# Stick-breaking attention: the eight heads worked in pairs instead of one after the other

## The reference, cut to what matters

```python
z = q @ k.T * hd ** -0.5
mask = key_pos < q_pos                       # strictly earlier keys
log_1mb = where(mask, log_sigmoid(-z), 0.0)
later = reverse_cumsum(log_1mb) - log_1mb    # over the keys
w = where(mask, exp(log_sigmoid(z) + later), 0.0)
out = w @ v
```

## Time and profile before

| | us |
|---|---|
| median of 3 runs (2521.0 to 2522.18) | 2521.75 |
| the profiled execution, its own time | 2521.97 |
| its span from first to last instruction | 2520.0 |
| first logits of the stage (L1310) | 1810.53 |
| copy of the last head's output (L2843) | 1923.59 |
| from one to the other | 113.06 |

### The profile page before, as it was taken

The page is one execution under the profiler, slowest core; times in us unless marked ns, Lnnn a source line. Parts: engine busy times, 40 slices in busy tenths (PEclk is TensorE's granted clock), DMA queues, the critical chain, the costliest instruction groups (busy, mean ns, idle before and its releaser), DMA issues.

```text
span 2520.0 us, 32191 instructions
## 1 busy us (share of the span) xinstructions
PE 2410.5 (96%) x12056; PEld 2069.8 (82%) x12056; DVE 1341.5 (53%) x1855; ACT 912.2 (36%) x1439; POOL 1087.3 (43%) x879
## 2 busy tenths in 40 slices
PE   5999889999999999999999999999888999999999
PEld 5899789999999998766788888888754766788887
DVE  7757866746565644889641222557444332543433
ACT  4222332313131323777632332345544343322322
POOL 1533132534444432378644567844520422444444
PEclk8999999999999999999999999999999999999999
DMA  6434012423333231411222322322300211232223
GB/s 246 150 101 140 28 59 70 149 101 117 117 109 114 102 111 43 132 33 44 69 84 92 104 97 80 113 84 92 117 17 6 76 59 56 78 101 93 100 92 109
DMA packets 71910, 232.04 MB, mean 92 GB/s; under 512 B 9824, under 2 KB 14048, under 8 KB 71776
## 3 DMA queue, kind: packets, MB, share of 16 engines
q1 hardware_dynamic: 71776, 230.16, 27.5%
HBM read 218.00 MB, written 2.10 MB: 87 GB/s over the span
## 4 chain that ended last, share of the span: by engine, by line
PE 78%; DVE 7%; POOL 5%; issue 5%; ACT 3%; DMA 1%; SPq 1%; POOLq 0%; DVEq 0%; ACTq 0%
PE PS L792 57%; PE PS L810 8%; PE PS L833 3%; POOL HL L592 2%; PE PS L1324 2%; POOL XR L634 1%; DVE RD L2640 1%; POOL PL L634 1%; PE PS L1425 1%; SPq L474 1%; PE PS L1310 1%; DMA EARLY<-adastream 1%; DVE OG L2454 1%; DVE SM L2624 1%; PE PS L892 0%
## 5 line engine op out<-in xcount | busy, mean ns | idle before, releaser
L592 POOL TENSOR_TENSOR HL<-RAW,HL 128x512 fp32r<-128x512 f32 x614 | 872.9, 1443 | 1303.9 <-ACT HL L1468 1302.7
L792 PE MATMUL PS<-HID,HL 128*128 128x384 f32 (+1 forms) x2832 | 562.1, 359 | 0.6 <-DVE HID L2196 0.6
L792 PE MATMUL PS<-HA,HL 128*128 128x512 f32 (+2 forms) x2592 | 552.0, 365 | 8.8 <-DVE VA L2563 2.3
L792 PEld LDWEIGHTS PS<-HID,HL 128*128 128x128 f32 x2832 | 509.5, 188 | 51.5 <-DVE HID L2196 1.1
L792 PE MATMUL PS<-HB,HL 128*128 128x512 f32 (+2 forms) x2592 | 538.9, 359 | 0.0
L792 PEld LDWEIGHTS PS<-HA,HL 128*128 128x128 f32 x2592 | 464.3, 189 | 74.4 <-issue 22.6
L792 PEld LDWEIGHTS PS<-HB,HL 128*128 128x128 f32 x2592 | 462.9, 188 | 50.7
L1468 ACT ACTIVATE HL<-RAW 128x1024 fp32r<-128x1024 f32 x307 | 323.3, 1054 | 476.4 <-PE PS L792 383.8
L2252 DVE CUSTOM_DVE_ANT_0 ADJ<-ADA,CB 128x1024 f32<-128x1024 f32 x160 | 264.3, 1652 | 12.8 <-DVE X L2172 5.2
L2172 DVE SCALAR_TENSOR_TENSOR X<-PS,MOD,X 128x256 f32<-128x256 f32 (+1 forms) x160 | 80.7, 546 | 285.2 <-PE PS L792 271.9
L2201 DVE TENSOR_TENSOR T<-T 128x768 f32<-128x768 f32 (+1 forms) x64 | 72.8, 1137 | 197.7 <-ACT T L1529 197.5
(11 more groups left out here) (421 smaller groups left out, 2583.4 us busy)
## 6 DMA issues: line engine op xcount, KB each, us to landing
RAW<-wstream SPq DMA_DIRECT2D x307, 512.0 KB, 3.3
ADA<-adastream SPq DMA_DIRECT2D x80, 512.0 KB, 3.8
EARLY<-adastream SPq DMA_DIRECT2D x16, 512.0 KB, 14.6
QB<-QH SPq DMA_DIRECT2D x32, 128.0 KB, 2.3
X<-x_in SPq DMA_DIRECT2D x8, 384.0 KB, 6.7
QC<-QL SPq DMA_DIRECT2D x16, 128.0 KB, 2.3
out<-X SPq DMA_DIRECT2D x8, 256.0 KB, 2.0
X<-mem SPq DMA_DIRECT2D x1, 1024.0 KB, 5.7
```

Source lines behind the costliest of these rows:

```text
L592: a = pool.tensor_tensor(HL[:, t % RING, 1, half], RAW[:, t % RAW_RING, half], HL[:, t % RING, 0, half].bitcast(F32), ALU.subtract)
L792: mm = pe.matmul(PS[:, bk, 0:hi - lo], w[:, wp, k * P:(k + 1) * P], a[:, ap, lo:hi], start=(k == 0 and (wp, ap) == (0, 0)), stop=(k == nk ...
```

## The change

- Heads are worked in pairs c = (2c, 2c+1), called a = 0 and a = 1. `sb_bank` gives six banks to a pair: block 0 of the two heads in banks 0 and 1, block 1 in banks 2 and 3, block 2 of both in bank 4, block 3 of both in bank 5.
- `logits(c)` issues the eight logit products of the pair so that head a = 0 (lower array half) and a = 1 (upper half) alternate, and two neighbours never go to the same bank. It starts when the weights of blocks 3 and 2 of the pair before are read, and waits inside for blocks 1 and 0. Eight masks follow.
- `later(c, 0)` and `later(c, 1)` are the same ten products each.
- ACT does six `Abs` (two of head 1, four of head 0), `Exp` and `Ln` of head 0, the other two `Abs`, `Exp` and `Ln` of head 1, and then the `Exp` of both heads' weights.
- DVE writes softplus over `AB` in place; the weights go to new tiles `WT`, so `SPB` goes.
- `values(c)` issues the eight products of the pair alternating between the two column halves, one pair late, and waits for all eight weights. `pair_out` copies them.
- The SSM has bank 7 alone: `state_in` comes in four parts of 8 passes. Parts 1 and 2 and `state_out(0)` stand between the last `later` of a pair and the next logits; part 3, `lag_products` and `state_out(1)` stand behind `values` in a pair.
- POOL computes its powers before the low parts of tiles `T_OUT2` to +2, and ACT makes one high part after each of the first three pairs. SP loads tile `T_OUT2` + 2 before the `LAG` moves and + 3 after them, and + 4 after the y moves.

```diff
+        SB_BANK, SB_COL = [(0, 1), (2, 3), (4, 4), (5, 5)], [(0, 0), (0, 0), (0, 256), (0, 128)]
+        def sb_bank(a, i, lo, hi=NX):
+            return PS[:, SB_BANK[i][a], SB_COL[i][a] + lo - i * P:SB_COL[i][a] + hi - i * P]
+        SB_LOGITS = [(0, 3), (1, 2), (0, 1), (1, 1), (0, 0), (1, 0), (1, 3), (0, 2)]
+        SB_MASKS = [(0, 3), (1, 3), (0, 2), (1, 2), (0, 1), (0, 0), (1, 1), (1, 0)]
...
+            def logits(c):
...
+                if c:
+                    pe.wait_ge(S("sb_weights"), 8 * c - 2)
+                for n, (a, i) in enumerate(SB_LOGITS):
+                    if c and n in (2, 4):
+                        pe.wait_ge(S("sb_weights"), 8 * c - n % 4 // 2)
+                    if n == 6:
+                        pe.wait_ge(S("sb_first"), 2 * c + 2)
+                    p, lo = slice(64 * a, 64 * a + 64), i * P
+                    mm = pe.matmul(sb_bank(a, i, lo), KS[p, c, lo:lo + P], QS[p, c, lo:NX], start=(n < 6), stop=True,
+                                   skip_group_check=True)
...
+                for a, i in SB_MASKS:
+                    pe.matmul(sb_bank(a, i, i * P, (i + 1) * P), const(C_ID), const(C_MS), start=False, stop=True,
+                              skip_group_check=True).then_inc(S("sb_logits"), 1)
...
+            def values(c):
+                if c:
+                    pe.wait_ge(S("sb_out"), c)
+                pe.wait_ge(S("sb_weights"), 8 * c + 8)
                 for i in (3, 2, 1, 0):
...
+                    for a in range(2):
+                        h = 2 * c + a
+                        mm = pe.matmul(PS[64 * a:64 * a + 64, 6, i * P:NX], VS[:, i, h * 64:h * 64 + 64],
+                                       WT[a][:, sb_part(i)], start=(i == 3), stop=(i == 0), skip_group_check=True)
...
+            logits(0)
+            conv_point(1)
+            state_in(0)
+            later(0, 0)
+            later(0, 1)
+            state_in(1)
+            logits(1)
+            values(0)
+            lag_products()
+            later(1, 0)
+            later(1, 1)
+            state_in(2)
+            logits(2)
+            values(1)
+            state_in(3)
+            later(2, 0)
+            later(2, 1)
+            state_out(0)
+            logits(3)
+            values(2)
+            state_out(1)
+            later(3, 0)
+            later(3, 1)
+            values(3)
...
+            def softplus(c, a):
+                dve.wait_ge(S("sb_ln"), 4 * c + 2 * a + 2)
+                if a:
+                    dve.wait_ge(S("sb_weights"), 8 * c + 2)
```

More of the change, by code:

```diff
@@ L739, in _ @@
             pool.sem_inc(S("powers"), 1)
[L741 removed]
+            lows(T_OUT2, LAST_TILE)
         @block.tensor
@@ L1298, in _ @@
             conv_point(0)
[L1300 to L1303, removed]
+            def logits(c):
+                if c == 0:
+                    pe.wait_ge(S("hm_scaled"), len(HEADS2.jobs))
+                    pe.wait_ge(S("bt_ready"), 4)
                     pe.wait_ge(S("free_V"), freed_by["V"][T_OUT2])
                     pe.wait_ge(S("free_A"), freed_by["A"][T_OUT2])
-                for i in (3, 2, 1, 0):
[L1307 to L1310, removed]
-                for i in (3, 2, 1, 0):
[L1312 to L1341, removed]
-                mm.then_inc(S("sb_summed"), 1)
@@ L1344, in _ @@
-            for h in range(SB_HEADS):
-                stick(h)
-            values(SB_HEADS - 1)
+                if c:
[8 more added lines that the diff above has]
+                                   skip_group_check=True)
+                    if n < 2:
+                        mm.then_inc(S("sb_first"), 1)
@@ new lines, in sb_abs, with sb_ln @@
+            def sb_abs(c, n):
+                a, i = SB_MASKS[n]
+                act.wait_ge(S("sb_logits"), 8 * c + (2 if n < 2 else 4 if n < 4 else n + 1))
+                return act.activation(AB[:, a, sb_part(i)], sb_bank(a, i, i * P), ACT.Abs)
+            def sb_ln(c, a):
+                act.wait_ge(S("sb_abs"), 2 * c + a + 1)
+                act.activation(AB[:, a], AB[:, a], ACT.Exp, scale=-1.0).then_inc(S("sb_ln"), 1)
+                act.wait_ge(S("sb_ln"), 4 * c + 2 * a + 1)
+                act.activation(AB[:, a], AB[:, a], ACT.Ln, bias=1.0).then_inc(S("sb_ln"), 1)
@@ new lines, in _ @@
+            act.wait_ge(S("hm_scaled"), len(HEADS2.jobs))
+            act.wait_ge(S("cv_act"), 1)
+            for c in range(SB_PAIRS):
+                for n in range(6):
+                    a = sb_abs(c, n)
+                a.then_inc(S("sb_abs"), 1)
+                sb_ln(c, 0)
+                for n in range(6, 8):
+                    a = sb_abs(c, n)
+                a.then_inc(S("sb_abs"), 1)
+                sb_ln(c, 1)
+                if c:
+                    act.wait_ge(S("sb_summed"), c)
+                if c == 3:
+                    state_copy(1)
+                sb_weights(c, 0)
+                if c == 1:
@@ L1939, in _ @@
                                    ACT.Copy).then_inc(S("act_once"), 1)
[L1940 to L1944, removed]
+                sb_weights(c, 1)
+                if c == 2:
+                    state_copy(0)
+                if c < AHEAD:
+                    high(t + c)
             def mix_square(k):
```

127 lines of the change are left out of this document (69 added, 58 removed).

## The result

The changed kernel takes 2484.81 us (median of 4 runs, 2480.77 to 2485.57) against 2521.4 (4 runs, 2521.0 to 2522.18). The ratio is 0.9851 with a 95% interval of 0.9834 to 0.9868: 1.5% faster, 36.6 us. The prediction said 2493.5, 28.2 us faster, with a range of 2487 to 2508.

A forecast was written before the change was run, and what follows sets the result against it. The bound was one head's path through three engines with no second head beside it. The stage, 4 x 18.4 + 6.3 + 3.7 = 83.6 against 113.06, minus 1.3, saved 28.2 us: 2493.5, range 2487 to 2508.

The forecast's parts named there:

- elementwise chain of 5.8 us: Abs, Exp, Ln and softplus work between logits and later products: stands once in a pair's path instead of twice.
- the 83.6: Forecast length in us of the stage from first logits to last copy, against 113.06 before.
- the 3,320 columns: Columns of a pair's logits left in line on PE after partial overlap of the array halves, 3.05 us.
- in-order pattern: Logits and values on PE: a product's second pass overlaps the other half's first, giving 3.05 and 2.83 us a pair.
- SSM on the path: state_in parts 1 and 2, state_out(0) and 1.7 us of state_out(1) overflowing its gap: 6.3 us in all.
- The end: After the last later products, values wait for all eight weights, then the copy: 3.7 us.
- the term of 1.3: Before the first logits, POOL's powers beside DVE slow the multiply on the path, costing 1.3 us.
- (1) No overlap: Array halves do not overlap in logits and values, 4.7 us each: 14 us more, 2507.5; chance 0.11.
- (2) The second y group late: Moves of the second y group start or land 6 us late before state_y(1), losing 3: 2497; chance 0.08.
- (3) Column halves pay for their loads: Weight loads of values do not overlap, values 6.9 us: about 16 us more, 2510; chance 0.03.
- (4) The clock: PE gets 1.2 instead of 2.4 GHz in the stage; throughout the kernel would take 2557; chance 0.04.
- I count no such dip after: No low-clock stretch in the stage after the change, as PE no longer idles long; one would cost 1.7 us.

The follow-up runs named there:

- one-chain kernel with dummies: Changed kernel with ACT's Exp and Ln of head 1 behind head 0's weights, plus seven dummy products on PE before head 1's later products: 2500.21 us.
- one-chain kernel: Changed kernel with ACT's Exp and Ln of head 1 issued behind the weights of head 0 instead of ahead of them: 2503.52 us.

## Why the prediction was partly right, point by point

**What bounds the stage.** Right. One head's path through PE, ACT, DVE and PE was the limit, and pairing the chains gave 15 us by experiment. The "elementwise chain of 5.8 us" is misread, though: by the prediction's own rows, from the end of the logits to "later" it is 5.1 (0.59 + 1.43 + 0.02 + 2.70 + 0.35), and 5.8 is the whole gain of a pair (24.17 less 18.4), the fold of the logits included. The baseline was also not clean: its 113.06 us hold two stretches of low clock, the one of head 7, which the prediction named and left in, and the one at 1818, which it overlooked. So part of the stage's 34.7 us, perhaps 2 to 4 (an estimate: 1.7 for the stretch of head 7, and the 2.1 by which the stage was shorter without the other), is not the new order's. What it left out is that PE becomes the limit: after the change PE idles about 1.05 us in pair 0, 0.41 and 0.34 in pairs 1 and 2, and 0.78 before the last values.

**The logits and values of a pair. This is the step of the mechanism that failed.** The miss has two parts, and either alone would have left the time in the range: the stage came out 5.2 us shorter than the 83.6 (the overlap of the halves and the terms below), and 4.0 us were gained ahead of it, a term that the prediction did not have at all (see "Outside the stage"). In the stage the largest mis-sized term is the overlap of the halves. I took the pattern "a product's second pass runs beside the other half's first" from the earlier trace rows and got 3.05 and 2.83 us. Measured: 2.35 and 2.31, the lower bound, which the prediction had given and not chosen. That is 0.70 in each of four pairs and 0.5 at the end, 3.3 us in all. (The seventh product of the order is of the same half as the sixth; the 3,320 columns allow for it, and it cost nothing either.) The experiments show that the halves are not tied to turns: even head after head they overlapped for the most part, and only a wait for completion made them serial (4.90 and 4.72). The trace of before had said it in the earlier trace rows: 32 passes over four column groups in 1.08 us is 3.5 times overlap, where the in-order pattern gives 17 steps of 0.12, 2.0 us. I weighed the case that resembled the new one and passed over the row that contradicted the pattern.

**Other terms of the pair.** "Later" 8.89 for two heads, not 9.28: in the one-chain kernel with dummies each head's took 4.55 (1843.07 to 1847.62), so the second head's, whose softplus is ready ahead of it, takes 4.34 here. First mask to `Abs` 0.75, not 0.86, and 5.03 from there to "later", not 5.2. Together with the logits the pair is 17.02, not 18.4, 5.5 us in four pairs. SSM on the path 6.0, not 6.3. The end 3.2, not 3.7, which is the values. Against it the low clock in the first pair, 1.1 more. 83.6 - 5.5 - 0.3 - 0.5 + 1.1 = 78.4, the measured stage.

**The beginning.** Wrong as a cause. POOL's powers hardly slowed the multiply in the trace after (1.27; 1.22 without), and by 0.4 at most in any other. The first logits did come later in relation to the projection, by 1.3: 7.55 us behind the start of the transposes (1800.33 to 1807.88), 6.24 before (1804.29 to 1810.53). Of this 0.4 is `conv_point` at a low clock, the rest lies in DVE's normalisation ahead of it, which ran more slowly beside POOL's low parts (3.25 instead of 2.17 us for its last two instructions). It comes and goes with the same program ahead of the stage: in five traces of the changed kernel's variants the same two took 2.15 to 2.16 us, and `conv_point(0)` started 4.5 us behind the transposes instead of 5.2. That the sum agrees with the term of 1.3 is chance.

**Outside the stage. This is the term that the prediction put at nothing, without a word.** It took all that lies ahead of the stage as unchanged. But the profiled execution before lost more time to low clock there (the stretches near 958, 1279 and 1641) than the one after, and the last projection products ended 4.0 us earlier. From the last copy to the end it is 596.4 before and 596.8 after. So the spans differ by 34.7 (stage) + 4.0 - 1.3 - 0.4 = 37.0; read, 36.9. Without the 4.0 us the time would have been near 2489, inside the range. Against the medians of 2519 that the kernel before had in the later runs the gain is some 35 us (35.8 for the changed kernel again), so the prediction's 28.2 was too small there too, and the stage accounts for most of it.

**The rivals.** (1) No overlap: false, and its price was right in kind: with the waits the logits cost 10.1 us more and the values 8.4, where the prediction had 14 for both, counted from 3.05 and 2.83. (2) The second y group late: no; it lands about 1891.2 (the last issue ends at 1889.4, plus 1.8), 2.4 us ahead of its use; I had a margin of 3. (3) Column halves pay for their loads: no. 16 passes with their 16 loads took 2.31 us. The rows of the kernel before already spoke against it: a head's 8 passes took no more than their 2,560 columns at 0.92 ns (2.35), with 8 loads of 0.136 on the same rows beside them. The Trainium skill, page "TensorEngine Tiling (Array Packing)", section "Key Properties", says that different tiles can load weights and multiply in parallel, and this trace agrees, for halves of 64 rows and of 64 columns. The rule cited in the prediction, of the Trainium skill's page "TensorE: Matmul & The Clock Gate", section "Part 3: Packing small matmuls — row/col tiling", that loads overlap only where the row group differs, does not hold here: the two column halves lie on the same rows. (4) The clock: mean 0.98 in the stage, not low. But "after an idle gap the clock fell" was right and stronger than I used it: 3.47 us idle brought a dip in each pair of the one-chain kernel. And "I count no such dip after" was wrong by 1.1 us: one fell in the first pair.

## What to carry to other kernels

Where one item walks through several engines with nothing beside it, a second one in flight takes the part that other engines do out of the path once in each pair (here 15 us for `Exp`, `Ln` and softplus), and the estimate comes straight from the chain of waits. Small products on separate halves of the array overlapped fully here when issued in turns, for about two thirds when issued half after half, and only a wait between them made them serial. And look at the stage in the trace, not only at the whole: whole times of one program spread over some 12 us with stretches of low clock that moved from run to run, more than most of the parts under test. For the same reason, look for such stretches in the baseline before a sum is built on it.

## What the runs showed of the hardware that I had not expected

- Products issued head after head, all of the lower array half first, still overlapped with the upper half's: 3.12 us for 5,120 columns where each half alone needs 2.35 (logits), and 3.0 (values). A product of the upper half ran before one of the lower half that stands ahead of it in the program.
- The same program's time varied from 2510.2 to 2523.05 us with low-clock stretches at places that differ from run to run; four earlier runs had been within 1.2 us.
- Idle PE costs twice: behind a wait of 3.47 us the next 4.5 us of work took 6.2, at a granted clock of 0.50 for part of it.
- When POOL and DVE work on SBUF at once, either may be the slow one: DVE's scans in the earlier trace rows (5.72 against 2.62 us), POOL's operations in the trace after (2.17 against 1.19).
